# Scale pieces first in the prologue of a two-layer hybrid backbone step

## The chip, the cores and the metric

The kernel runs on one core of a Trainium2 chip. The metric is the device time of one execution in microseconds (us), lower is better. Engines are called as in the profile: PE is TensorE (PEld its weight loads), DVE is VectorE, ACT is ScalarE, POOL is GpSimd, SP is SyncE, which here only issues DMAs.

## What is computed

A trunk of two layers is applied to 512 latent tokens and 128 context tokens of width 1024. Each layer begins with an RMS norm whose result is scaled and shifted by a modulation (adaLN). The modulation is a vector of 6 x 1024 numbers per group of tokens, worked out from a small input vector by a matrix of 1024 x 6144:

```
mod = (jax.nn.silu(c) @ ada_w[l] + ada_b[l])[:, None, :]
xs, _ = _trunk_layer(xs, mod, layers[l], ctx)
```

Inside the layer the input of the first projection is, in effect, `rms_norm(x) * norm1_g * (1 + scale) + shift`, with shift the first 1024 and scale the second 1024 numbers of the modulation. DeltaNet, latent attention, window attention, an output projection and an MLP follow. The change touches only how this first modulation of layer 0 is made ready.

## The kernel before, in words

All matrix products of the layers are run as three products of rounded halves: a weight chunk `RAW` (128 x 2048) is rounded by ACT to `HI` (`split_hi`, L602) and DVE writes the rest `RAW - HI` to `LO` (`split_lo`, L927). The input is treated the same way: `X` is scaled by `GAIN` and rounded by ACT to `HH` (`norm_hi`, L607, two instructions for each of 8 tiles k: 128x512 for the latent tokens, 128x128 for the context tokens), and DVE writes `X * GAIN - HH` to `HL` (`norm_lo`, L934, again two instructions for each k). The shift does not go into X: it is one extra column at the end of `HH` and `HL` (`shift_hi` L614, `shift_lo` L944), so a projected tile brings its own bias. PE's `wstat` (L1409) multiplies; for its first tile it waits for the shift columns (semaphore `h_sl`), for the first `LO`, and before each k for `norm_lo` of that k (semaphore `h_lo`).

The modulation needed first (shift and scale of layer 0, 2048 numbers) comes in 8 pieces of 1 MB, `ADA`, 256 numbers each; pieces 0 to 3 are shift and 4 to 7 scale. For each piece j PE multiplies it (`ada_half`, L321, 16 matmul records), DVE copies the row from PSUM to `MODB` (L963), and PE turns the row into columns of PSUM bank 7 (`ada_turn`, L328, 4 records). PE's program runs `ada_half(j)` and then `ada_turn(j-1)`; `ada_half(j)` waits for the copy of j-1, which DVE signals by `pro_ev`. After the last turn DVE adds the bias (`ada_bias`, L334), makes `GAIN` (`ada_gain`, L339), and the normalised input follows.

POOL starts when X has landed and computes sums of squares of X for the RMS norm (`square_sum`: one L482, then seven pairs of L484 and L486, two SBUF inputs each), 15 instructions. Their result is used by PE only after its first tile.

Order is fixed by the program of each engine and by semaphores; nothing is scheduled by a table. All DMAs of this stretch are issued by SP in one queue in program order.

Of the kernel before, what the change touches and what calls it, by code (L numbers as in the profile page):

```python
# [15 lines left out]
KT = D // P  # L16
# [109 lines left out]
def build(nc, t):  # L126

    ctx = ExitStack()
    with ctx:
# [122 lines left out]
        def bank(i):  # L252
            return PS[:, i, :]
# [71 lines left out]
        def ada_turn(pe, rows, at_):  # L325

            for q in range(2):
                last = pe.matmul(bank(7)[:, 4 * at_ + 2 * q:4 * at_ + 2 * q + 2], rows[:, toks(q)], sel,  # L328
                                 start=True, stop=True)
            return last  # L330

        def ada_bias(lo, hi, vec):

            return nc.vector.tensor_tensor(MOD[:, lo:hi, :], bank(7)[:, 0:2 * (hi - lo)].rearrange("p (j g) -> p j g", g=2),  # L334
                                           vec.unsqueeze(2).broadcast_to([P, hi - lo, 2]), ALU.add)

        def ada_gain(q, sc, vec):

            return nc.vector.scalar_tensor_tensor(out=GAIN[:, q, :, :], in0=MOD[:, sc:sc + KT, :], scalar=1.0,  # L339
                                                  in1=vec.unsqueeze(2).broadcast_to([P, KT, 2]),  # L340
                                                  op0=ALU.add, op1=ALU.mult)

        pro_buf = [4, 5, 6, 7, 8, 0, 1, 2]
        blocks = [[LB if s == LB else (s if d == 0 else LB - 1 - s) for d in range(2)] for s in range(NB)]


# [3 lines left out]
        with nc.Block() as block:  # L350

            @block.sync
            def _(sp):
# [1 line left out]
                sp.dma_start(VA[:, :], t["va"][0]).then_inc(setup, 16)  # L355
                sp.dma_start(FG[:, :], t["fg"]).then_inc(setup, 16)
                for j in range(8):
                    if j == 2:
                        sp.dma_start(K[:, :], t["K"]).then_inc(k_in, 16)
                    if j == 3:  # L360
                        sp.dma_start(X[:, :, :, :], t["xT"]).then_inc(x_in, 16)
                    if j == 6:
                        sp.dma_start(RAW[0][:, :], t["ws"][0]).then_inc(raw_in[0], 16)
                    sp.dma_start(ADA[pro_buf[j]][:, :, :], t["ada"][0, j]).then_inc(pro_in[j], 16)
                sp.dma_start(RAW[1][:, :], t["ws"][1]).then_inc(raw_in[1], 16)

                def refill(g):
# [229 lines left out]
            def _(act):  # L597

                def split_hi(g):

                    act.wait_ge(raw_in[g % 2], 16 * (g // 2 + 1))
                    nc.scalar.copy(HI[g % 2][:, :], RAW[g % 2][:, :]).then_inc(hi_ready, 1)  # L602

                def norm_hi(q, k):

                    for g in range(2):
                        last = nc.scalar.activation(grp(HH[:, k, :, :], g), grp(X[:, k, :, :], g), ACT.Identity,  # L607
                                                    scale=GAIN[:, q % 2, k, g:g + 1])
                    last.then_inc(S["h_hi"], 1)

                def shift_hi(q):

                    lo = 3 * KT * (q % 2)
                    nc.scalar.copy(HH[:, :, 0, HT:W1], MOD[:, lo:lo + KT, :]).then_inc(S["h_sh"], 1)  # L614
# [7 lines left out]

                act.wait_ge(c_in, 16)
                nc.scalar.activation(SC[:, :, :], SC[:, :, :], ACT.Silu).then_inc(silu_c, 1)
                split_hi(0)
                act.wait_ge(k_in, 16)
                act.wait_ge(setup, 32)
                act.wait_ge(x_in, 16)
                act.wait_ge(pro_mod, 2)
                shift_hi(0)  # L630
                for k in range(KT):
                    norm_hi(0, k)
                for l in range(DEPTH):
                    o, g0 = base(l), l * CHUNKS

# [279 lines left out]
            def _(dve):  # L915
# [43 lines left out]
                for j in range(8):  # L959
                    dve.wait_ge(pro_mm, j + 1)  # L960
                    if j >= 2:
                        dve.wait_ge(pro_tr, j - 1)
                    nc.vector.tensor_copy(MODB[j % 2][:, :], bank(6)[:, j % 2 * AC:(j % 2 + 1) * AC]).then_inc(pro_ev, 1)  # L963
                    if j == 6:
                        split_lo(0)
                dve.wait_ge(pro_tr, 8)
                dve.wait_ge(setup, 32)
                ada_bias(0, 2 * KT, VA[:, 0:2 * KT]).then_inc(pro_mod, 1)
                dve.wait_ge(pro_mod, 1)
                ada_gain(0, KT, VA[:, 2 * KT:3 * KT]).then_inc(pro_mod, 1)  # L970
                shift_lo(0)
                dve.wait_ge(pro_mod, 2)
                for k in range(KT):
                    norm_lo(0, k)
                for l in range(DEPTH):
                    o, g0 = base(l), l * CHUNKS

# [412 lines left out]
            def _(pe):  # L1390
# [34 lines left out]
                    last.then_inc(nrb, 1)  # L1425

                pe.wait_ge(silu_c, 1)
                pe.wait_ge(k_in, 16)
                for j in range(9):
                    if j < 8:  # L1430
                        pe.wait_ge(pro_in[j], 16)
                        if j:
                            pe.wait_ge(pro_ev, j)
                        ada_half(pe, pro_buf[j], j).then_inc(pro_mm, 1)
                    if j:
                        pe.wait_ge(pro_ev, j)
                        ada_turn(pe, MODB[(j - 1) % 2], j - 1).then_inc(pro_tr, 1)
                used = [0] * 4
                for l in range(DEPTH):
                    o, g0, t0 = base(l), l * CHUNKS, l * TILES  # L1440
# [504 lines left out]
```

## Time and profile before

| what | value |
| --- | --- |
| time, median of 3 runs | 2066.24 us (2066.21 to 2070.67) |
| profiled execution: its own time | 2064.92 us |
| profiled execution: span in the trace | 2063.1 us |
| PE busy (share of the span) | 1954.9 us (95%) |
| DVE, ACT, POOL busy | 973.7, 663.7, 446.2 us |
| PE idle before its first `wstat` matmul | 5.22 us, first matmul at 45.43 us |

The span is the time from the first to the last record of the trace; the execution's own time is 1.8 us longer. PE is busy nearly always once the layers run. What matters here is the first 46 us, in which PE works little.

### The profile page before, as it was taken

The page shows a single profiled execution, that of the slowest core. Times are in us where ns is not written, and L with a number is a line of the kernel's source. Part 1 is how long each engine was busy: PE and PEld are TensorE (multiplying, and loading weights), DVE is VectorE, ACT ScalarE, POOL GpSimd, SP SyncE. Part 2 cuts the span into 40 slices and gives each one's busy share as a digit, 9 for nine tenths or more (in the row PEclk, how much of TensorE's full clock was granted, in tenths as well). Part 3 has the DMA queues.
Part 4 walks back from the last instruction along what each step waited for, and adds up shares of the span by engine and source line. Part 5 has one row for each costly group of instructions (what it writes and reads, how often), then busy time and mean ns, then how long its engine had stood idle before and what let it go on. Part 6 is the DMA issues. An engine that isn't in the chain of part 4 may idle for free. (4 is left out here: it accounts for less than half of the span.)

```text
span 2063.1 us, 32862 instructions
## 1 busy us (share of the span) xinstructions
PE 1954.9 (95%) x14279; PEld 1833.3 (89%) x14279; DVE 973.7 (47%) x1422; ACT 663.7 (32%) x1009; POOL 446.2 (22%) x326
## 2 busy tenths in 40 slices
PE   5999989897999999999999999989989999999996
PEld 3999966787999999999999998668879999999996
DVE  3445755677642323232555467457765332323223
ACT  2444246312322231312335432661122413122221
POOL 4000010342332030312430000013323403121144
PEclk9999999999999999999999999999999999999998
DMA  8444120101142222212254432010022122122111
GB/s 339 146 162 156 62 68 1 37 1 57 62 163 103 85 82 80 82 63 81 82 196 164 149 111 76 14 37 1 1 77 82 62 82 82 62 82 82 62 62 51
DMA packets 45630, 177.85 MB, mean 86 GB/s; under 512 B 21072, under 2 KB 22864, under 8 KB 26032
## 3 DMA queue, kind: packets, MB, share of 16 engines
q1 hardware_dynamic: 43952, 174.29, 23.9%
q8 instruction: 113, 1.85, 0.4%
q10 hardware_dynamic: 1536, 1.48, 0.2%
q14 instruction: 29, 0.24, 0.0%
HBM read 166.98 MB, written 8.68 MB: 85 GB/s over the span
## 5 line engine op out<-in xcount | busy, mean ns | idle before, releaser
L1409 PE MATMUL PS<-HH,HI 128*128 128x322 f32 (+1 forms) x1792 | 421.6, 317 | 5.2 <-DVE HL L934 5.2
L1409 PE MATMUL PS<-HL,HI 128*128 128x322 f32 (+1 forms) x1792 | 416.3, 314 | 0.0
L1409 PE MATMUL PS<-HH,LO 128*128 128x322 f32 (+1 forms) x1792 | 415.4, 313 | 0.0
L602 ACT CAST HI<-RAW 128x2048 fp32r<-128x2048 f32 x96 | 182.8, 1905 | 532.2 <-PE PS L1409 495.8
L1409 PEld LDWEIGHTS PS<-HH,HI 128*128 128x128 f32 x1792 | 304.5, 192 | 9.5 <-issue 9.4
L1409 PEld LDWEIGHTS PS<-HH,LO 128*128 128x128 f32 x1792 | 307.3, 192 | 0.0
L1409 PEld LDWEIGHTS PS<-HL,HI 128*128 128x128 f32 x1792 | 306.4, 192 | 0.0
L1409 PE MATMUL PS<-FH,HI 128*128 128x320 f32 x1280 | 292.9, 310 | 0.0
L1409 PE MATMUL PS<-FH,LO 128*128 128x320 f32 x1280 | 291.8, 309 | 0.0
L927 DVE TENSOR_TENSOR LO<-RAW,HI 128x2048 fp32r<-128x2048 f32 x96 | 231.7, 2414 | 105.6 <-ACT HI L602 105.6
L1409 PE MATMUL PS<-FL,HI 128*128 128x320 f32 x1152 | 263.2, 310 | 0.0
L583 POOL TENSOR_TENSOR TC<-TC 128x640 f32<-128x640 f32 x64 | 91.6, 1431 | 622.5 <-ACT FH L880 622.5
L956 DVE COPY BI<-PS 128x2 f32<-128x2 f32 x112 | 17.9, 160 | 425.7 <-PE PS L1409 412.9
L1409 PEld LDWEIGHTS PS<-FH,LO 128*128 128x128 f32 x1280 | 214.6, 188 | 0.0
L1409 PEld LDWEIGHTS PS<-FH,HI 128*128 128x128 f32 x1280 | 214.5, 189 | 0.0
L1335 DVE SCALAR_TENSOR_TENSOR X<-PS,MOD,X 128x512 f32<-128x512 f32 (+1 forms) x160 | 80.7, 546 | 262.1 <-PE PS L1409 262.1
L1409 PEld LDWEIGHTS PS<-FL,HI 128*128 128x128 f32 x1152 | 193.4, 188 | 0.0
L876 ACT ACTIVATE TC<-TMP,BI 128x512 f32<-128x512 f32 (+1 forms) x128 | 65.0, 555 | 201.1 <-DVE TMP L957 201.1
L586 POOL TENSOR_TENSOR FL<-TC,FH 128x640 fp32r<-128x640 f32 x64 | 100.1, 1564 | 5.0
L508 POOL COPY KTT<-KTT 32x1536 f32<-32x1536 f32 x2 | 4.0, 1982 | 448.8 <-DVE KTT L1129 448.8
L957 DVE TENSOR_TENSOR TMP<-PS,RB 128x640 f32<-128x640 f32 x112 | 91.3, 815 | 0.2 <-issue 0.2
L833 ACT COPY TT<-PS 128x512 f32<-128x512 f32 x40 | 21.7, 589 | 180.0 <-PE PS L1737 180.0
(270 smaller groups left out, 2458.5 us busy)
## 6 DMA issues: line engine op xcount, KB each, us to landing
RAW<-ws SPq DMA_DIRECT2D x96, 1024.0 KB, 4.8
ADA<-ada SPq DMA_DIRECT2D x48, 1024.0 KB, 5.0
X<-xT SPq DMA_DIRECT2D x1, 2560.0 KB, 16.5
X<-xT SPq DMA_DIRECT2D x2, 1280.0 KB, 5.7
xs<-X SPq DMA_DIRECT2D x1, 2560.0 KB, 8.4
X<-xs SPq DMA_DIRECT2D x2, 1280.0 KB, 5.9
yT<-YB SPq DMA_DIRECT2D x8, 320.0 KB, 2.2
ROT<-rot SPq DMA_DIRECT2D x2, 1024.0 KB, 4.8
```

The costliest lines, as they stand in the source:

```text
L508: nc.gpsimd.tensor_copy(KTT[64:QH, 1:H, 0:LAT], KTT[64:QH, 0:1, 0:LAT].broadcast_to([KR, H - 1, LAT])).then_inc(S["krc"], 1)
L583: nc.gpsimd.tensor_tensor(TC[u][:, 0:T], TC[u][:, 0:T], TC[u][:, 0:T], ALU.mult).then_inc(S["f1_sq"], 1)
L586: nc.gpsimd.tensor_tensor(flat(FL[:, e % 8, :, :]), TC[u][:, 0:T], flat(FH[:, e % 8, :, :]).bitcast(F32), ALU.subtract).then_inc(S["f1_lo" ...
L602: nc.scalar.copy(HI[g % 2][:, :], RAW[g % 2][:, :]).then_inc(hi_ready, 1)
L833: nc.scalar.copy(TT[d][:, :, :], bank(4 * d + 3).rearrange("p (h c) -> p h c", h=H)).then_inc(S["tcp"], 1)
L876: last = nc.scalar.activation(grp(TC[u][:, 0:T].rearrange("p (a b) -> p a b", a=2), g), grp(TMP[u][:, :, :], g), ACT.Relu, bias=BI[:, n % ...
L927: nc.vector.tensor_tensor(LO[g % 2][:, :], RAW[g % 2][:, :], HI[g % 2][:, :].bitcast(F32), ALU.subtract).then_inc(lo_ready, 1)
L956: nc.vector.tensor_copy(BI[:, n % 4, :], PS[:, 2 * (n % 2), HT:W1])
L957: nc.vector.tensor_tensor(TMP[n % 2][:, :, :], even(n % 2), RB[:, :, :], ALU.mult).then_inc(S["w_ev"], 1)
L1335: last = nc.vector.scalar_tensor_tensor(out=x, in0=grp(even(n % 2), g), scalar=MOD[:, gate + k, g:g + 1], in1=x, op0=ALU.mult, op1=ALU.add)
L1409: last = pe.matmul(bank(2 * u + a)[:, 0:e], w[:, cols], m[:, a, 0:e], start=(k == 0 and f), stop=(k == KT - 1 and e_))
```

## The change

The 8 pieces are loaded and worked through in the order 4, 5, 6, 7, 0, 1, 2, 3 (`pro_seq`), so scale comes before shift. X and the first weight chunk are both issued behind the fourth piece. DVE makes bias and gain of the scale part after the fourth turn, and puts `norm_lo` two at a time, and `split_lo(0)`, between its copies of the last four rows. ACT starts `norm_hi` when the gain is there and puts `split_hi(0)` in its middle. The shift part gets its own bias instruction at the end. PE waits for the constants `K` (which hold the selector matrix of the turns) only at its first turn.

```
         def ada_bias(lo, hi, vec):
 
-            return nc.vector.tensor_tensor(MOD[:, lo:hi, :], bank(7)[:, 0:2 * (hi - lo)].rearrange("p (j g) -> p j g", g=2),
+            at_ = 2 * lo if hi <= 2 * KT else 0
+            return nc.vector.tensor_tensor(MOD[:, lo:hi, :], bank(7)[:, at_:at_ + 2 * (hi - lo)].rearrange("p (j g) -> p j g", g=2),
                                            vec.unsqueeze(2).broadcast_to([P, hi - lo, 2]), ALU.add)
...
         pro_buf = [4, 5, 6, 7, 8, 0, 1, 2]
+        pro_seq = [4, 5, 6, 7, 0, 1, 2, 3]
...
                 for j in range(8):
-                    if j == 2:
+                    sp.dma_start(ADA[pro_buf[j]][:, :, :], t["ada"][0, pro_seq[j]]).then_inc(pro_in[j], 16)
+                    if j == 0:
                         sp.dma_start(K[:, :], t["K"]).then_inc(k_in, 16)
                     if j == 3:
                         sp.dma_start(X[:, :, :, :], t["xT"]).then_inc(x_in, 16)
-                    if j == 6:
                         sp.dma_start(RAW[0][:, :], t["ws"][0]).then_inc(raw_in[0], 16)
-                    sp.dma_start(ADA[pro_buf[j]][:, :, :], t["ada"][0, j]).then_inc(pro_in[j], 16)
                 sp.dma_start(RAW[1][:, :], t["ws"][1]).then_inc(raw_in[1], 16)
...
-                split_hi(0)
                 act.wait_ge(k_in, 16)
                 act.wait_ge(setup, 32)
                 act.wait_ge(x_in, 16)
                 act.wait_ge(pro_mod, 2)
+                for k in range(KT):
+                    if k == 4:
+                        split_hi(0)
+                    norm_hi(0, k)
+                act.wait_ge(pro_mod, 3)
                 shift_hi(0)
-                for k in range(KT):
-                    norm_hi(0, k)
...
+                    if j == 3:
+                        dve.wait_ge(pro_tr, 4)
+                        dve.wait_ge(setup, 32)
+                        ada_bias(KT, 2 * KT, VA[:, KT:2 * KT]).then_inc(pro_mod, 1)
+                        dve.wait_ge(pro_mod, 1)
+                        ada_gain(0, KT, VA[:, 2 * KT:3 * KT]).then_inc(pro_mod, 1)
+                        dve.wait_ge(pro_mod, 2)
+                    if j >= 4:
+                        norm_lo(0, 2 * (j - 4))
+                        norm_lo(0, 2 * (j - 4) + 1)
                     if j == 6:
                         split_lo(0)
                 dve.wait_ge(pro_tr, 8)
-                dve.wait_ge(setup, 32)
-                ada_bias(0, 2 * KT, VA[:, 0:2 * KT]).then_inc(pro_mod, 1)
-                dve.wait_ge(pro_mod, 1)
-                ada_gain(0, KT, VA[:, 2 * KT:3 * KT]).then_inc(pro_mod, 1)
+                ada_bias(0, KT, VA[:, 0:KT]).then_inc(pro_mod, 1)
+                dve.wait_ge(pro_mod, 3)
                 shift_lo(0)
-                dve.wait_ge(pro_mod, 2)
-                for k in range(KT):
-                    norm_lo(0, k)
...
                 pe.wait_ge(silu_c, 1)
-                pe.wait_ge(k_in, 16)
...
                         pe.wait_ge(pro_ev, j)
-                        ada_turn(pe, MODB[(j - 1) % 2], j - 1).then_inc(pro_tr, 1)
+                        if j == 1:
+                            pe.wait_ge(k_in, 16)
+                        ada_turn(pe, MODB[(j - 1) % 2], pro_seq[j - 1]).then_inc(pro_tr, 1)
```

On DVE, from the copy of the fourth row on, the program before reads as follows (the numbers behind the names tell buffers apart; MODB_115 and MODB_116 are the two row buffers):

```order
L963 COPY MODB_116<-PS 128x256
L963 COPY MODB_115<-PS 128x256
L963 COPY MODB_116<-PS 128x256
L963 COPY MODB_115<-PS 128x256
L927 TENSOR_TENSOR LO_55<-RAW_51,HI_53 128x2048
L963 COPY MODB_116<-PS 128x256
L334 TENSOR_TENSOR MOD<-PS,VA 128x32
L339 SCALAR_TENSOR_TENSOR GAIN<-MOD,VA 128x16
L944 TENSOR_TENSOR HL<-MOD,HH 128x8x2
L934 SCALAR_TENSOR_TENSOR HL<-X,GAIN,HH 128x2x256
```

On DVE after the change, from the same copy of the fourth row to the copy of the sixth:

```order
L966 COPY MODB_116<-PS 128x256
L335 TENSOR_TENSOR MOD<-PS,VA 128x16
L340 SCALAR_TENSOR_TENSOR GAIN<-MOD,VA 128x16
L966 COPY MODB_115<-PS 128x256
L937 SCALAR_TENSOR_TENSOR HL<-X,GAIN,HH 128x2x256
L937 SCALAR_TENSOR_TENSOR HL<-X,GAIN,HH 128x2x64
L937 SCALAR_TENSOR_TENSOR HL<-X,GAIN,HH 128x2x256
L937 SCALAR_TENSOR_TENSOR HL<-X,GAIN,HH 128x2x64
L966 COPY MODB_116<-PS 128x256
```

Four `norm_lo` instructions now stand between one copy and the next; the same four stand behind the next two copies, the second of them with `split_lo(0)` after it, and the last four behind the last copy.

On SP, the queue before, from the first piece to the second chunk (ADA_110 is the buffer of the first piece in order, RAW_51 the first weight chunk):

```order
L364 DMA ADA_110<-ada 128x2048
L364 DMA ADA_111<-ada 128x2048
L359 DMA K<-K 128x1924
L364 DMA ADA_112<-ada 128x2048
L361 DMA X<-xT 128x5120
L364 DMA ADA_113<-ada 128x2048
L364 DMA ADA_114<-ada 128x2048
L364 DMA ADA_106<-ada 128x2048
L363 DMA RAW_51<-ws 128x2048
L364 DMA ADA_107<-ada 128x2048
L364 DMA ADA_108<-ada 128x2048
L365 DMA RAW_52<-ws 128x2048
```

The same queue after the change:

```order
L360 DMA ADA_110<-ada 128x2048
L362 DMA K<-K 128x1924
L360 DMA ADA_111<-ada 128x2048
L360 DMA ADA_112<-ada 128x2048
L360 DMA ADA_113<-ada 128x2048
L364 DMA X<-xT 128x5120
L365 DMA RAW_51<-ws 128x2048
L360 DMA ADA_114<-ada 128x2048
L360 DMA ADA_106<-ada 128x2048
L360 DMA ADA_107<-ada 128x2048
L360 DMA ADA_108<-ada 128x2048
L366 DMA RAW_52<-ws 128x2048
```

X has moved behind one more piece, the first chunk ahead of two pieces more; the bytes ahead of the last piece are the same.

On PE the order of instructions does not change; the row of the fourth turn stands where it stood, behind the half of the fifth piece (ADA_114):

```order
L321 MATMUL PS<-ADA_113,SC 32x256 x8
L328 MATMUL PS<-K,MODB_115 128x2 x2
L321 MATMUL PS<-ADA_114,SC 32x256 x8
L328 MATMUL PS<-K,MODB_116 128x2 x2
L321 MATMUL PS<-ADA_106,SC 32x256 x8
```

The second turn shown here (MODB_116) is that of the fourth piece, for which the gain now waits.

## Rows read from the trace of the kernel before

**Rows 1.** The page: busy time of each engine, share of the span, instructions.

```profile
PE 1954.9 (95%) x14279; PEld 1833.3 (89%) x14279; DVE 973.7 (47%) x1422; ACT 663.7 (32%) x1009; POOL 446.2 (22%) x326
```

**Rows 2.** Timeline of PE: start us, duration us, group, [idle before <- releaser].

```profile
33.19 1.94 PE L321 MATMUL PS<-ADA,SC 128*32 128x256 f32 x16 [1.45 <-DMA ADA<-ada]
35.05 1.01 PE L328 MATMUL PS<-K,MODB 128*128 128x2 f32 x4
39.20 1.01 PE L328 MATMUL PS<-K,MODB 128*128 128x2 f32 x4 [0.33 <-DVE MODB L963]
45.43 0.88 PE L1409 MATMUL PS<-HH,HI 128*128 128x322 f32 x2 [5.22 <-DVE HL L934]
```

**Rows 3.** Timeline of ACT, 28 to 60 us.

```profile
30.69 1.90 ACT L602 CAST HI<-RAW 128x2048 fp32r<-128x2048 f32 x1 [27.42 <-DMA RAW<-ws]
41.67 0.21 ACT L614 CAST HH<-MOD 128x16 fp32r<-128x16 f32 x1 [9.09 <-DVE GAIN L339]
41.78 7.34 ACT L607 ACTIVATE HH<-X,GAIN 128x512 fp32r<-128x512 f32 x16
```

**Rows 4.** Timeline of DVE, 34 to 60 us, and its instruction at 42.91 alone.

```profile
35.53 3.28 DVE L927 TENSOR_TENSOR LO<-RAW,HI 128x2048 fp32r<-128x2048 f32 x1
38.73 0.41 DVE L963 COPY MODB<-PS 128x256 f32<-128x256 f32 x1
40.25 0.19 DVE L334 TENSOR_TENSOR MOD<-PS,VA 128x32 f32<-128x32 f32 x1 [1.10 <-PE PS L328]
40.48 1.09 DVE L339 SCALAR_TENSOR_TENSOR GAIN<-MOD,VA 128x16 f32<-128x16 f32 x1
41.91 0.98 DVE L944 TENSOR_TENSOR HL<-MOD,HH 128x16 fp32r<-128x16 f32 x1 [0.35 <-ACT HH L614]
42.91 8.86 DVE L934 SCALAR_TENSOR_TENSOR HL<-X,GAIN,HH 128x512 fp32r<-128x512 f32 x16
51.68 2.28 DVE L927 TENSOR_TENSOR LO<-RAW,HI 128x2048 fp32r<-128x2048 f32 x1
42.91 2.12 DVE L934 SCALAR_TENSOR_TENSOR HL<-X,GAIN,HH 128x512 fp32r<-128x512 f32 x1
```

**Rows 5.** Timeline of POOL, 20 to 45 us.

```profile
20.78 1.25 POOL L482 TENSOR_TENSOR SQA<-X 128x640 f32<-128x640 f32 x1 [20.33 <-DMA X<-xT]
36.74 3.18 POOL L484 TENSOR_TENSOR TC<-X 128x640 f32<-128x640 f32 x1
40.00 1.53 POOL L486 TENSOR_TENSOR SQA<-SQA,TC 128x640 f32<-128x640 f32 x1
41.61 1.25 POOL L484 TENSOR_TENSOR TC<-X 128x640 f32<-128x640 f32 x1
42.94 1.53 POOL L486 TENSOR_TENSOR SQA<-SQA,TC 128x640 f32<-128x640 f32 x1
```

**Rows 6.** Timeline of DVE and POOL later in the program.

```profile
543.33 1.25 POOL L484 TENSOR_TENSOR TC<-X 128x640 f32<-128x640 f32 x1 [3.81 <-DVE X L1335]
544.34 0.79 DVE L934 SCALAR_TENSOR_TENSOR HL<-X,GAIN,HH 128x512 fp32r<-128x512 f32 x1 [1.16 <-ACT HH L607]
544.34 2.37 DVE L934 SCALAR_TENSOR_TENSOR HL<-X,GAIN,HH 128x512 fp32r<-128x512 f32 x2 [1.16 <-ACT HH L607]
544.66 1.89 POOL L486 TENSOR_TENSOR SQA<-SQA,TC 128x640 f32<-128x640 f32 x1
1010.82 3.49 POOL L486 TENSOR_TENSOR SQA<-SQA,TC 128x640 f32<-128x640 f32 x1
1012.81 2.31 DVE L934 SCALAR_TENSOR_TENSOR HL<-X,GAIN,HH 128x512 fp32r<-128x512 f32 x2
```

**Rows 7.** Busy time in two windows of the first tile, with granted clock (PEclk).

```profile
core 0: us, PE busy (x) PEld busy (x) DVE busy (x) ACT busy (x) POOL busy (x), PEclk, DMA share, GB/s
45.40:51.20 5.80, 5.77 (x22) 5.80 (x23) 5.80 (x13) 5.51 (x10) 0.00 (x0) 1.00 0.72 302
51.20:55.20 4.00, 4.00 (x27) 4.00 (x27) 2.77 (x3) 0.00 (x0) 2.04 (x2) 1.00 0.20 29
```

## The prediction, made before the changed kernel ran

> **What bounds the kernel now.** The page comes first: PE is busy 95% of the span [rows 1], so time is won or lost where PE waits. The timeline of PE then shows where that is in the stretch of the change: its last turn runs from 39.20 to 40.21, and its first real matmul starts at 45.43, after 5.22 us of waiting for a `norm_lo` [rows 2]. From there it runs without a gap. So what the change is worth is the shift of that one start, 45.43.
>
> What stands between the last piece and that start is read from the timelines of ACT, DVE and POOL. `ada_half` of the seventh piece starts when that piece lands, 33.19; the first chunk, one place ahead in the queue, lands at 30.69 [rows 2, 3]. So 1 MB takes 2.5 us. I take the transfers of this queue to run back to back at that pace, so that where a piece lands follows from its place in the queue. The eighth lands by 35.7. Its row is copied at 38.73 only, because `split_lo(0)` holds DVE from 35.53 on; then come turn (to 40.21), bias 0.19, gain 1.09, `shift_hi` 0.21, `shift_lo` 0.98 and the first `norm_lo` 2.12 and 0.26 [rows 3, 4].
>
> The reader is to see that three of these durations are not work. The gain is issued at 40.48 and ends at 41.57, just behind a POOL instruction that ends at 41.53. `shift_lo` ends at 42.89 behind one that ends at 42.86. The first `norm_lo` ends at 45.03, 0.56 behind one that ends at 44.47. The other way round, `split_lo(0)` ends at 38.81 and the POOL instruction under way from 36.74 takes 3.18 in place of 1.25 [rows 4, 5]. The bias and the copies, which read PSUM and at most one SBUF tensor, are not held. So DVE instructions with two SBUF inputs and POOL's take turns, each waiting for the whole of the other. POOL is done at 44.5; seven and a half of the eight `norm_lo` run behind that, free, at 0.93 us for each k (45.29 to 51.77), well ahead of PE.
>
> Who goes next when both want to is read further on. At 544.34 DVE issues the two instructions of a `norm_lo`. The first goes when POOL's ends at 544.58, POOL's next (issued 544.66) follows and ends at 546.55, and DVE's second ends at 546.71: it waited for all of POOL's. At 1010.82 a POOL instruction waits behind a `split_lo`; it then runs to 1014.31 ahead of a `norm_lo` pair issued at 1012.81, which takes 2.31 [rows 6]. A waiting POOL instruction gets in between any two of DVE's.
>
> **The change, step by step.** Landings: cvec to the eighth piece are the same bytes. K, X and the chunk change places with pieces. X lands one piece later, so POOL starts at 20.78 + 2.5 = 23.3. The chunk lands at about 25.7, pieces five to eight at 28.2, 30.7, 33.2, 35.7, the last as before.
>
> *The gain.* The first four pieces (scale) are in at about 17 (28.2 less a piece 2.5, the chunk 2.5 and X, 2.5 MB, 6.2) and their rows copied at about 20. But PE's program puts the fourth turn behind the half of the fifth piece, which lands at 28.2. A turn ends 2.87 behind the start of the half in front of it (33.19 to 36.06 [rows 2]): 31.1. The gain is issued at 31.3 and waits for a POOL instruction that ends at 31.6 (the L484 three pairs ahead of the one at 36.74 began at 36.74 - 3 x 2.95 = 27.89; + 2.5 + 1.25 [rows 5]). So the gain is there at 31.7, 9.9 ahead of 41.57; that is what the change brings.
>
> *What is now put between the copies.* On POOL are left from 31.7 on one L486 and four pairs L484/L486. Each pair takes 2.95 undisturbed (from the end of L482 at 22.0 to 36.74 are five pairs). A 128x512 `norm_lo` taking its turn costs POOL 1.89 - 1.53 = 0.35 [rows 5, 6] and the second none; so in contention one k takes 2.95 + 0.35 = 3.3 in place of 0.93. ACT starts `norm_hi` at 31.8 at 0.92 each (7.34 / 8 [rows 3]), fast enough.
>
> - Copy 5 at 31.8 to 32.2 (its row is there at 30.2); half 6 at 32.3, its row at 34.3.
> - `norm_lo` 0: POOL's L486 ends at 33.3, pair one gives 33.8 for the first instruction and 35.1 for the second. `norm_lo` 1: 3.3 later, 38.4.
> - Copy 6 at 38.4 to 38.8, 4.1 behind its row. As `ada_half` of the next piece waits for this copy, half 7 starts at 38.9, though its piece landed at 33.2.
> - `norm_lo` 2 and 3 wait for POOL first (39.9), two more cycles: 45.0. Copy 7 to 45.5, half 8 at 45.6, its row at 47.5.
> - `norm_lo` 4: POOL's last ends at 46.5, then free: 47.3; `norm_lo` 5: 48.2; `split_lo(0)` without POOL (2.28, as the one at 51.68 [rows 4]): 50.4.
> - Copy 8 to 50.8, turn 50.9 to 51.9. That is 11.7 behind 40.21.
> - Behind the last turn less is left: `norm_lo` 6 and 7 end at 52.6, shift bias 52.8, `shift_hi` 53.1, `shift_lo` 53.3 with POOL gone (some 0.2, by the bias's 0.19). PE starts 0.1 later at 53.4. That tail is 1.5 where it was 5.2.
>
> Sum: + 11.7 - 3.7 = + 8.0 us; the start goes from 45.4 to 53.4. The one added bias costs 0.2 and is in it. K's wait moved behind the first half lets PE begin earlier at the very start only, where it next waits for pieces anyway: nothing.
>
> *What hangs behind.* `split_hi(1)` and `split_lo(1)` follow 4 us after the start and are wanted only two tiles later. SP's refill waits for `split_lo(0)` (now 50.4, before 38.8), and queued behind it are the parameters and the next two `ADA` loads, some 5 us each; they are wanted after the first tile (before: 55.2 [rows 7], now 63). POOL's sums end at 46.5 and are wanted at 63. All covered. So everything after moves by the same 8.0. Cover lost anywhere here would cost at most what is late: the parameters would have to land over 7 us later than the 56 expected.
>
> *Clock.* In the first 5.8 us of the first tile PE finishes 22 matmuls in 5.77, or 0.262 each; then 27 in 4.00, or 0.148, at a granted clock of 1.00 in both windows [rows 7]. So the first matmuls run at about half speed, that is, as at 1.2 GHz, the lower of the clock's two levels, though the column says 1.00. Before the start PE had idled 5.2 us; after the change it idles 1.5 us with a thin pattern ahead. I take the same slow stretch. If it were gone, 5.8 us of work would take 3.3: 2.5 less. If the rest of the tile (27 matmuls) were slow too: 3.1 more.
>
> **A rule beside the row.** The row gives 3.3 us for one contended k: POOL's pair of 2.95 and 0.35 for the DVE instruction that took its turn, since the two overlap at their edges [rows 5, 6]. The Trainium skill, page "SBUF — State Buffer", section "Who interferes with whom", speaks against this change: a DVE instruction with two SBUF inputs and a GpSimd one that reads SBUF exclude each other for their whole length. Taken at its word, a contended k is the sum of both engines' durations, 2.95 + 0.93 = 3.9, and the four contended ones add 2.3 us more: a start at 55.7, + 10.3, where the row gives + 8.0. The row decides.
>
> **Bounds of the contention.** Low: DVE keeps the port while it has instructions and POOL waits, rival one. High: from 31.7 on nothing overlaps: all of POOL's remaining work (1.5 + 4 x 2.8 = 12.7), DVE's 16 `norm_lo` 7.4, `split_lo(0)` 2.3, four copies 1.7 and the shift part 0.7 add up to a start at 56.5, + 11.1. I take 8.0, since the rows at 544 and 1010 show the turn-taking itself.
>
> **Rivals.**
> - *DVE keeps its turn.* For it: in the back-to-back stretch before, instructions of DVE overlap by a few hundredths, so that POOL may not get in. Against: both places in rows 6. Then each `norm_lo` pair takes 1.9 to 2.7 with at most one POOL instruction between copies: copies 6, 7, 8 at 34.9, 37.8, 43.3; last turn to 44.8; `norm_lo` 6 and 7 and `shift_lo` behind POOL's rest: start at 48.1, + 2.7 us, 2068.9.
> - *The work is hidden, as the change wants.* The place is the gap of 2.5 us between two copies (half 1.94 and turn 1.01 less a copy 0.41). If POOL does not get in the way and `split_lo(0)` fits too, the last turn ends at about 39.4 and only bias, `shift_hi`, and `shift_lo` (waiting once for POOL) are left: start at 41.0, - 4.4 us, 2061.8. It decides once the four `norm_lo` instructions between copies take under 2.5; they take 1.9 free and 6.6 in turns. Against it is also `split_lo(0)`, which alone outgrows the gap.
> - *Clock.* As the main case, but PE starts fast: + 5.5, 2071.7.
>
> **How the numbers follow.** Turn-taking as worked out 0.72, DVE keeps its turn 0.12, hidden 0.06, clock 0.10. The sum is made in the profiled execution: 2064.92 + 8.0 = 2072.9 there (span 2071.1). The median of the runs is 1.3 above it, so 2066.24 + 8.0 = 2074.2. Range: the high end is the bound of + 11.1, 2077.3, rounded up to 2077.5; the low end takes in the first rival with little to spare, 2067.5; left out are the hidden case and the tails, under 0.2. About what a measurement of this kernel can tell from no change is 0.3%, 6.2 us. The main case lies 1.8 above that, and I give it 9 in 10 to stay above: 0.65, and 0.01 of the clock case for slower; the rest, with both other rivals, is same; faster by over 6.2 would need more than the hidden case gives: 0.02.
>
> **What would show it.** Right: gain at about 31.7; `norm_lo` instructions of 1.2 to 1.7 us each alternating with POOL's until 46 or 47; copies at 38.4, 45.0 and 50.4; PE's fourth, sixth and seventh waits inside the prologue ended by DVE's copies, not by DMAs; first `wstat` matmul at 53.4. Wrong: copies 6 and 7 on time at 34 and 37, POOL's instructions stretched in DVE's place, or the gain at 20 (if the fourth turn were not held by the fifth piece). A first matmul at 0.148 each from the start would show the clock case.

## The result, and the profile after

The changed kernel takes 2073.09 us (median of 22 runs, 2066.62 to 2082.78), the kernel before 2066.22 us in the same series (22 runs, 2056.1 to 2074.59). The ratio is 1.0032 with a 95% interval of 1.0019 to 1.0045: slower by 6.6 us, 3.9 to 9.3. The profiled execution took 2072.92 us with a span of 2071.1. Ratios here and below leave out slow executions; there was one, of the spread version, of 8153.11 us.

Of the timeline of PE in the changed kernel these are the rows from the fifth piece on that end a wait; they answer to [rows 2].

```profile
28.04 1.94 PE L321 MATMUL PS<-ADA,SC 128*32 128x256 f32 x16 [7.56 <-DMA ADA<-ada]
32.06 1.94 PE L321 MATMUL PS<-ADA,SC 128*32 128x256 f32 x16 [1.15 <-DVE MODB L966]
38.61 1.94 PE L321 MATMUL PS<-ADA,SC 128*32 128x256 f32 x16 [3.67 <-DVE MODB L966]
45.15 1.93 PE L321 MATMUL PS<-ADA,SC 128*32 128x256 f32 x16 [3.66 <-DVE MODB L966]
50.47 1.01 PE L328 MATMUL PS<-K,MODB 128*128 128x2 f32 x4 [2.44 <-DVE MODB L966]
52.92 0.90 PE L1417 MATMUL PS<-HH,HI 128*128 128x322 f32 x2 [1.44 <-DVE HL L947]
...
62.40 1.17 PE L1425 MATMUL PS<-K,SQA 128*128 128x1 f32 x10
```

Before, what PE's halves waited for from there on was a landing piece (1.45 us at 33.19 [rows 2]). Now only the half at 28.04 waits for one. The three behind it, and the last turn, wait for a copy on DVE (1.15, 3.67, 3.66, 2.44 us). The last turn ends at 51.48 where it ended at 40.21, the first `wstat` matmul starts at 52.92 in place of 45.43, 7.5 us later. The sums of squares, the first thing after the first tile, come at 62.40.

The timeline of DVE, for [rows 4]:

```profile
31.16 0.29 DVE L340 SCALAR_TENSOR_TENSOR GAIN<-MOD,VA 128x16 f32<-128x16 f32 x1
31.49 0.42 DVE L966 COPY MODB<-PS 128x256 f32<-128x256 f32 x1
32.62 5.51 DVE L937 SCALAR_TENSOR_TENSOR HL<-X,GAIN,HH 128x512 fp32r<-128x512 f32 x4 [0.71 <-ACT HH L608]
38.05 0.41 DVE L966 COPY MODB<-PS 128x256 f32<-128x256 f32 x1
38.39 6.28 DVE L937 SCALAR_TENSOR_TENSOR HL<-X,GAIN,HH 128x512 fp32r<-128x512 f32 x4
44.59 0.41 DVE L966 COPY MODB<-PS 128x256 f32<-128x256 f32 x1
44.93 2.95 DVE L937 SCALAR_TENSOR_TENSOR HL<-X,GAIN,HH 128x512 fp32r<-128x512 f32 x4
47.80 2.28 DVE L930 TENSOR_TENSOR LO<-RAW,HI 128x2048 fp32r<-128x2048 f32 x1
50.00 0.41 DVE L966 COPY MODB<-PS 128x256 f32<-128x256 f32 x1
50.33 1.93 DVE L937 SCALAR_TENSOR_TENSOR HL<-X,GAIN,HH 128x512 fp32r<-128x512 f32 x4
```

The four `norm_lo` instructions (two k) take 5.51 and 6.28 us while POOL works, 2.95 where POOL ends in their midst, 1.93 when it is gone. From 32.62 to 52.3 DVE is never idle. The timeline of POOL, for [rows 5]:

```profile
23.08 1.25 POOL L483 TENSOR_TENSOR SQA<-X 128x640 f32<-128x640 f32 x1 [22.63 <-DMA X<-xT]
...
33.13 1.58 POOL L485 TENSOR_TENSOR TC<-X 128x640 f32<-128x640 f32 x1
34.79 1.54 POOL L487 TENSOR_TENSOR SQA<-SQA,TC 128x640 f32<-128x640 f32 x1
36.40 1.58 POOL L485 TENSOR_TENSOR TC<-X 128x640 f32<-128x640 f32 x1
...
44.60 1.54 POOL L487 TENSOR_TENSOR SQA<-SQA,TC 128x640 f32<-128x640 f32 x1
```

L485 starts at 33.13, 36.40, 39.68 and 42.94, every 3.27 us; undisturbed it was every 2.95. Of DVE's instructions two, taken alone, show the turns (start, duration):

```profile
34.78 2.09 DVE L937 SCALAR_TENSOR_TENSOR HL<-X,GAIN,HH 128x512 fp32r<-128x512 f32 x1
...
36.79 1.33 DVE L937 SCALAR_TENSOR_TENSOR HL<-X,GAIN,HH 128x128 fp32r<-128x128 f32 x1
```

The first, 128x512, was started at 34.78, just before POOL's L487 at 34.79, and took 2.09: it ends at 36.87, 0.54 behind POOL's end at 36.33. The second, 128x128, took 1.33 and ends at 38.12, 0.14 behind the end of L485 (36.40 + 1.58). Each waited until a POOL instruction had ended; 0.75 and 0.34 are their durations with POOL gone.

### The profile page after: what moved, and what is told of

Read it like the earlier page. It is cut to its first block and busy times, and to the rows that moved or that the text cites. A ratio compares the mean times of both kernels' runs of the same rounds, so it can differ in the third digit from the quotient of the medians.

```text
span 2071.1 us, 32864 instructions
## 1 busy us (share of the span) xinstructions
PE 1955.8 (94%) x14279; PEld 1834.5 (89%) x14279; DVE 979.7 (47%) x1423; ACT 663.8 (32%) x1009; POOL 446.4 (22%) x326
## 5 line engine op out<-in xcount | busy, mean ns | idle before, releaser
L321 PE MATMUL PS<-ADA,SC 128*32 128x256 f32 x768 | 58.3, 426 | 26.1 <-DMA ADA<-ada 17.6
```

Of the source, the lines that this page charges most:

```text
L321: last = pe.matmul(bank(6)[q:q + 32, j % 2 * AC:(j % 2 + 1) * AC], SC[:, k, :], ADA[buf][:, k, :], start=(k < 4), stop=(k >= 4))
```

## Experiments

Ten kernels in twelve runs. In each one the start of the first `wstat` matmul (before 45.43, changed 52.92) is what is compared; it and the rows around it are read in one trace. Transfers mostly land up to 0.4 us earlier or later from trace to trace, so a difference of that size is not read as an effect. The time of a single run says little either, as the last section shows.

### POOL's sums held back in the changed kernel

```
                 pool.wait_ge(x_in, 16)
+                pool.wait_ge(S["h_sl"], 1)
                 square_sum(0, lambda k: flat(X[:, k, :, :]))
```

> The changed kernel, with POOL's sums of squares of X held until shift_lo of the first norm is done; nothing else is moved. Theory (turn-taking between POOL and DVE makes the copies late): norm_lo pairs take 1.9 us between copies in place of 5.5 to 6.3, copies 6, 7, 8 come at about 34, 37 and 42, the last turn ends at 43.5 and the first wstat matmul starts at 45.2 in place of 52.9. Rival (DVE's own added work is what makes the copies late, POOL is no matter): the start stays at 52 to 53. In either case PE then waits some 13 us after its first tile for the sums, which end only at about 69, so the whole kernel is not faster than the changed one: about 2078.

DVE's timeline of this kernel:

```profile
32.77 1.94 DVE L938 SCALAR_TENSOR_TENSOR HL<-X,GAIN,HH 128x512 fp32r<-128x512 f32 x4 [0.71 <-ACT HH L609]
34.63 0.42 DVE L967 COPY MODB<-PS 128x256 f32<-128x256 f32 x1
34.97 1.93 DVE L938 SCALAR_TENSOR_TENSOR HL<-X,GAIN,HH 128x512 fp32r<-128x512 f32 x4
37.18 0.42 DVE L967 COPY MODB<-PS 128x256 f32<-128x256 f32 x1 [0.29 <-PE PS L321]
...
42.26 0.42 DVE L967 COPY MODB<-PS 128x256 f32<-128x256 f32 x1
```

The `norm_lo` groups take 1.94 and the copies come at 34.6, 37.2 and 42.3. The first `wstat` matmul starts at 45.18, as the theory said to 0.02 us. PE then waits 14.32 us for the sums, and the one run took 2083.9 us (about 2078 expected). Without POOL the changed prologue is only as good as the old one with POOL. That does not put the whole 7.5 us down to POOL, since the old one was held up by it too: see the run with POOL held back in the kernel before, where the loss is divided.

### The turn of the fourth piece early

```
                 for j in range(9):
+                    if j == 4:
+                        pe.wait_ge(pro_ev, 4)
+                        ada_turn(pe, MODB[1], pro_seq[3]).then_inc(pro_tr, 1)
                     if j < 8:
                         pe.wait_ge(pro_in[j], 16)
...
-                    if j:
+                    if j and j != 4:
                         pe.wait_ge(pro_ev, j)
```

That is the second form. In the first, the turn stood behind `pe.wait_ge(pro_in[j], 16)` and the wait for `pro_ev` that follows it.

> The changed kernel, with PE's turn of the fourth piece put ahead of the half of the fifth, so that the gain no longer waits for a piece that lands at 28. Both theories: gain at about 20.9 in place of 31.4. Theory (DVE with its port waits is the bound from 31 on): norm_lo still stands behind copy 5, which comes 1.1 us earlier, so the start moves from 52.9 to about 51.7 only. Rival (the late gain is what spoils the change): the start follows the gain by up to 10 us, to 43 to 46.

In the first form the turn ran at 27.94, behind the wait for the fifth piece, and the gain ended at 30.05: the edit did not do what it was meant to. The start moved to 52.64.

> The changed kernel, with PE's turn of the fourth piece now ahead of the wait for the fifth piece too (in the first attempt it stood behind that wait and moved by one half only). Gain at about 20.9, ACT's norm_hi from X's landing at 23 on. Theory (from copy 5 on DVE and POOL share one port, and their work adds up): copy 6 at 36.8, copy 7 at 43.3, but POOL's sums then end as late as before and take from norm_lo 4 and 5 what was won; start at 52.4, 0.5 below the changed kernel. Rival (the late gain is what spoils the change): start at 43 to 46.

Mended, the gain ended at 22.06, 9.4 us ahead of the changed kernel. The start was 52.87, unchanged within 0.05 (expected 52.4), and the one time 2075.15. X landed 0.3 us later in this trace (POOL began at 23.37, not 23.08), so some 0.3 of the 0.5 forecast may be there. DVE's timeline shows why:

```profile
21.89 0.17 DVE L340 SCALAR_TENSOR_TENSOR GAIN<-MOD,VA 128x16 f32<-128x16 f32 x1
...
37.02 0.41 DVE L966 COPY MODB<-PS 128x256 f32<-128x256 f32 x1
37.36 6.28 DVE L937 SCALAR_TENSOR_TENSOR HL<-X,GAIN,HH 128x512 fp32r<-128x512 f32 x4
43.56 0.41 DVE L966 COPY MODB<-PS 128x256 f32<-128x256 f32 x1
43.90 3.94 DVE L937 SCALAR_TENSOR_TENSOR HL<-X,GAIN,HH 128x512 fp32r<-128x512 f32 x4
...
49.96 0.41 DVE L966 COPY MODB<-PS 128x256 f32<-128x256 f32 x1
```

Copies 6 and 7 come 1.0 us earlier than in the changed kernel, but the group behind copy 7 takes 3.94 in place of 2.95, and copy 8 is at 49.96 in place of 50.00. POOL's sums end when they end (46.8 and 46.1); what DVE does ahead of that, it pays for. The rival, a late gain, falls for the changed kernel: the gain came 9.4 us earlier and 0.3 us at most followed.

### The `norm_lo` back behind `shift_lo`

```
-                    if j >= 4:
-                        norm_lo(0, 2 * (j - 4))
-                        norm_lo(0, 2 * (j - 4) + 1)
...
                 shift_lo(0)
+                for k in range(KT):
+                    norm_lo(0, k)
```

> The changed kernel, with the eight norm_lo put back behind shift_lo; order of loads, early gain and early norm_hi stay. Theory (what stands between the copies does the harm): copies come on their rows, copy 8 at about 40.5, the last turn ends at 41.7, POOL still overlaps until 46 to 47, the start is at 45 to 46, as before the change. Rival (the new order of the loads, with X one piece later, does the harm): the start stays above 50.

Copy 8 came at 39.74, the last turn ended at 41.47, the start was at 44.67, a little under the 45 to 46 expected and 0.8 ahead of the kernel before. The order of the loads is not what does the harm. But the eight `norm_lo` now took 11.10 us (before 8.86 [rows 4]), since POOL worked on until 47.64 (before 44.47); PE ran dry once more in its first tile:

```profile
44.67 0.87 PE L1416 MATMUL PS<-HH,HI 128*128 128x322 f32 x2 [3.20 <-DVE HL L937]
47.85 0.90 PE L1416 MATMUL PS<-HH,HI 128*128 128x322 f32 x2 [1.23 <-DVE HL L937]
```

and the sums came at 56.62, 1.3 us behind the kernel before (55.35). Its single time, 2078.59, is above what that explains: at the mark that stands at 203.03 in the trace before (explained in the last section) it was 2.8 us behind, at the one at 551.15 it was 11.5, so most of it arose later.

### `split_lo(0)` behind the last copy

```
-                    if j == 6:
+                    if j == 7:
                         split_lo(0)
```

> The changed kernel, with split_lo(0) moved from ahead of copy 8 to behind it and the last four norm_lo. Theory (DVE is busy or held without a gap from 32.6 to 52.3, so only the sum of its work counts): copy 8 comes at about 47.8 in place of 50.0, but the start stays at 52.9 within 0.3. Rival (the late last row and its turn set the start): the start comes 2.2 us earlier, at 50.7.

Copy 8 came at 47.75, 2.25 us earlier, the last turn ended at 49.24, and the start stayed at 52.87. So the late copies of the changed kernel are a sign, not the cause: DVE's work and the turns it waits for add up without a gap, and its last instruction sets the start.

### X and K first, in the kernel before and in the changed one

```
+                sp.dma_start(X[:, :, :, :], t["xT"]).then_inc(x_in, 16)
+                sp.dma_start(K[:, :], t["K"]).then_inc(k_in, 16)
                 for j in range(8):
...
-                        sp.dma_start(K[:, :], t["K"]).then_inc(k_in, 16)
...
-                        sp.dma_start(X[:, :, :, :], t["xT"]).then_inc(x_in, 16)
```

> The kernel before the change, with X and then K loaded ahead of the first piece; nothing else is moved. POOL's sums then run from about 11 to 33 and are done before split_lo(0), gain, shift_lo and norm_lo. Theory (POOL's turn-taking is on the path before, too): split_lo(0) 2.3 in place of 3.28, gain 0.3 in place of 1.09, shift_lo 0.2 in place of 0.98, first norm_lo 0.75 in place of 2.12; the last piece lands as before, at 35.7; the first wstat matmul starts at 41.6 in place of 45.4, and the time falls by 3.8 us. Rival (these waits are covered by something else): the start stays at 45 and the time is the same.

POOL now ended at 33.2. DVE's timeline of the kernel before with X first:

```profile
35.90 2.28 DVE L925 TENSOR_TENSOR LO<-RAW,HI 128x2048 fp32r<-128x2048 f32 x1
38.37 0.42 DVE L961 COPY MODB<-PS 128x256 f32<-128x256 f32 x1 [0.19 <-PE PS L321]
40.13 0.19 DVE L334 TENSOR_TENSOR MOD<-PS,VA 128x32 f32<-128x32 f32 x1 [1.34 <-PE PS L328]
40.36 0.17 DVE L339 SCALAR_TENSOR_TENSOR GAIN<-MOD,VA 128x16 f32<-128x16 f32 x1
40.88 0.18 DVE L942 TENSOR_TENSOR HL<-MOD,HH 128x16 fp32r<-128x16 f32 x1 [0.35 <-ACT HH L612]
41.88 7.49 DVE L932 SCALAR_TENSOR_TENSOR HL<-X,GAIN,HH 128x512 fp32r<-128x512 f32 x16 [0.82 <-ACT HH L605]
```

`split_lo(0)` took 2.28 (3.28), the gain 0.17 (1.09), `shift_lo` 0.18 (0.98), each as the theory had it or better. The start was 43.04, not 41.6: 2.4 us gained, not 3.8. Three things were missed. Piece seven landed 0.36 us later than before (its half began at 33.55, not 33.19), and the last half with it (36.37, not 35.99). With copy 8 on time, the last turn queues on PE behind the one before it (8 records in 1.87 us, to 40.10), so the last turn ended only 0.1 ahead of the 40.21 of before. And the first `norm_lo` waits 0.82 for ACT's first `norm_hi`, which was hidden behind `shift_lo` held by POOL. The ratio to the kernel before was 0.9983 (0.9963 to 1.0002). A second series:

> The kernel before with X and K first, once more, beside the spread version on the same chip: start at 43.0, time 2.4 to 2.9 us below the kernel before, 1.5 above the spread version if that starts at 41.5.

Start at 42.90, the ratio 0.9990 (0.9970 to 1.0011); the medians, 2064.15 and 2063.13 for the kernel before, stand the other way round. The difference is in the trace both times and under what the times can show.

> The changed kernel, with X and K loaded ahead of the first piece. POOL is done at about 33, so only the first norm_lo meets it. Theory: start at about 45.3, the time 7.6 us below the changed kernel and that of the kernel before within 1 us; so without any contention the change still gives nothing, because DVE's own work between the copies (1.9 and 4.1 us against gaps of 2.5) makes them late, and against the kernel before with X first it loses 3.7 us. Rival (contention was all that spoiled the change): start at 41 or earlier, time below 2062.5.

The start was 46.95: 6.0 us ahead of the changed kernel, but 1.5 behind the kernel before and 3.9 behind the same loads in the old order of work. (1.2 of the distance from the expected 45.3 is the gain, which met POOL's last instruction and took 1.45.) The ratio was 1.0011 (0.9992 to 1.0031), and the median 2065.9 us against 2059.91 for the old order with X first in the same series. DVE met POOL no more in its `norm_lo`, and in the trace the change still lost against the old order. The first two gaps held their 1.9 us of work (copy 7 came as soon as its row was there); the third did not hold 0.58 of waiting for ACT, 1.9 and 2.3, so copy 8 came at 44.03, 2.3 behind its row, and the last four `norm_lo` stand ahead of the shift.

### POOL held back in the kernel before

```
                 pool.wait_ge(x_in, 16)
+                pool.wait_ge(S["h_lo"], KT)
```

> The kernel before the change, with POOL's sums of squares held until the eighth norm_lo of the first norm is done, loads as they were. Theory: the same four waits go, and the start moves from 45.4 to about 41.5 even with X landing late, so that it is POOL and not the place of X in the queue. Rival (the place of X in the queue matters by itself): the start stays at 45. Either way PE waits about 19 us for the sums after its first tile, so the kernel is slower.

The gain took 0.17, `shift_lo` 0.18, `split_lo(0)` 2.28, again. The start was 43.87, less than hoped; the last piece landed late in this run (the half waited 0.88 us for it and began at 37.19, before 35.99), and from the start of that half to the first `wstat` matmul are 6.68 us, where it was 9.44 and, with X first, 6.67 (36.37 to 43.04). So holding POOL back and loading X first give the same; it is POOL, not the place of X. PE waited 20.69 us for the sums; the one time was 2089.56.

With this the 7.5 us can be divided. Without POOL the changed kernel started at 45.18. The kernel before without POOL would have started at 42.67, had its last half begun at 35.99 as before (an estimate: 35.99 + 6.68). So sharing with POOL costs the changed kernel 7.7 us (52.92 less 45.18) and the kernel before 2.8 (45.43 less 42.67): 5.0 more. The other 2.5 (45.18 less 42.67) are the new order of DVE's work itself.

### Work spread by what the gaps hold

X and K first as above, scale first, the early turn, and:

```
                 nc.scalar.activation(SC[:, :, :], SC[:, :, :], ACT.Silu).then_inc(silu_c, 1)
+                split_hi(0)
...
                         ada_gain(0, KT, VA[:, 2 * KT:3 * KT]).then_inc(pro_mod, 1)
+                        split_lo(0)
                         dve.wait_ge(pro_mod, 2)
-                    if j >= 4:
-                        norm_lo(0, 2 * (j - 4))
-                        norm_lo(0, 2 * (j - 4) + 1)
-                    if j == 6:
-                        split_lo(0)
+                    for k in {4: (0,), 5: (1, 2), 6: (3, 4), 7: (5,)}.get(j, ()):
+                        norm_lo(0, k)
...
                 shift_lo(0)
+                norm_lo(0, 6)
+                norm_lo(0, 7)
```

> X and K first, scale pieces first, the turn of the fourth piece ahead of the fifth half, split_hi(0) ahead of norm_hi, split_lo(0) right behind the gain, then one, two, two and one norm_lo behind copies 5, 6, 7, 8, and the last two behind shift_lo, where PE's slow start hides them. Theory (each gap between copies holds about 2.5 us of DVE work, and what does not fit there goes behind the start): gain at about 27.4, copies within 1 us of their rows, last turn ends at 39.8, start at 40.6 to 41.5, the time 4 to 5 us below the kernel before (about 2061.5). Rival (the copies are made late again): start above 43.

This had the turn in its first form, behind the wait for the fifth piece. Gain at 30.10, start at 43.31, ratio 1.0000 (0.9980 to 1.0020). That is the rival's number (above 43), but not for its reason alone: copies 5 and 6 were 0.9 and 0.7 us behind their rows, copies 7 and 8 on time, and the gain was 2.7 us late, since the early turn was missing.

> The spread version with the turn of the fourth piece ahead of the wait for the fifth. Theory: gain at 26 to 27, copies 5 to 8 within 1 us of their rows, last turn ends near 40.7, start at 41.5, 1.8 below the first spread version and 3.9 below the kernel before; the time 3.9 us below the kernel before. Rival (POOL's last two or three instructions and split_lo(0) still push copy 5 and all behind it): start at 43 as in the first version.

```profile
28.53 1.94 PE L321 MATMUL PS<-ADA,SC 128*32 128x256 f32 x16 [0.44 <-DMA ADA<-ada]
...
37.64 1.93 PE L321 MATMUL PS<-ADA,SC 128*32 128x256 f32 x16 [0.33 <-DVE MODB L964]
39.51 1.87 PE L328 MATMUL PS<-K,MODB 128*128 128x2 f32 x8
42.16 0.90 PE L1415 MATMUL PS<-HH,HI 128*128 128x322 f32 x2 [0.78 <-DVE HL L945]
...
51.18 1.06 PE L1423 MATMUL PS<-K,SQA 128*128 128x1 f32 x9
```

Gain at 28.53, two later than expected: the first half begins only at 16.18, when its piece has landed behind X and `K`, and four halves and turns follow it nearly without a gap; copies within 1 us of their rows; the last turn ends at 41.38, the start is at 42.16 (expected 41.5), the sums at 51.18: 3.3 and 4.2 us ahead of the kernel before. Ratio 0.9982 (0.9962 to 1.0003). Run once more:

> The mended spread version once more, for its time. Theory: start at 42.2 and end of the first tile at 51.2 again, 4.2 us ahead of the kernel before, and the time 3 to 4 us below it (ratio 0.998 to 0.9985). Rival (what is won in the first 55 us is lost again further on): ratio within 0.0005 of 1.

Start at 42.17, the sums at 51.89; ratio 0.9991 (0.9974 to 1.0008), medians 2062.56 and 2066.22 us; the end of the first tile was 3.5 us ahead, not 4.2, and the ratio lies between what the theory and the rival had. Both intervals lie below that of the changed kernel (1.0019 to 1.0045), so this version beats it. Against the kernel before the trace shows 3.3 us in the start, and the times can't tell it from nothing. The rival is not ruled out: the last section follows the lead through the traces.

## Why the prediction was right

The forecast was 2074.2 us and + 8.0; measured were 2073.09 and + 6.9 between the medians. By its steps:

- **Landings and gain.** Right. X's first use at 23.08 (23.3), the half of the fifth piece at 28.04 (28.2), gain at 31.45 (31.7).
- **Turn-taking.** Right, and the size too: 3.27 us for a contended k (3.3). The 128x512 `norm_lo` costs POOL 0.33 and the 128x128 one nothing. Only the sign for it was drawn too narrow: single instructions took 0.98 to 2.09 us with their waits, not 1.2 to 1.7. The Trainium skill's reading in the prediction (page "SBUF — State Buffer", section "Who interferes with whom"), with both durations in full, gave 3.9 and a start at 55.7. That two-input instructions exclude each other agrees with the trace; that their whole durations add does not (3.27, not 3.9), since they overlap by their edges.
- **Copies and last turn.** 38.05, 44.59, 50.00 and 51.48 (38.4, 45.0, 50.4, 51.9): the difference of 0.4 is there from copy 6 on, and 0.25 of it from the first `norm_lo`, which found POOL's instruction ending at 33.05, not 33.3.
- **The tail.** 1.44 (1.5).
- **The sum.** The start moved by 7.5 (8.0). The first tile took 9.48 in place of 9.92, so its end moved by 7.05. The medians differ by 6.9, but their agreement with this is partly luck: the interval of 3.9 to 9.3 would hold 5 or 8 as well.
- **The bounds and rivals.** DVE does not keep its turn. The hidden case was reached by no kernel tried. From the start of the last half to the end of the last turn passed 3.73 us with X first and 3.74 in the spread version, so a turn ending at 39.4 needs that half to start with its piece, at 35.7. In the spread version, the best one, it waited for copy 7 and began at 37.64; the start was 42.16.

What the prediction had in the wrong light is the path. It followed the late copies from piece to piece, as if PE and DVE passed a delay to and fro. Moving `split_lo(0)` took 2.25 us from the last copy and nothing from the start, and a gain 9.4 us earlier gave 0.3 at most: from 32.6 on the bound is DVE with its turns. The steps summed right because they listed all of DVE's work anyway.

That the span of the profiled execution came out at just the forecast 2071.1 is chance: the first tile ended 7.05 later, POOL's first `UU` at 378.90 before came at 388.42 (+ 9.5), and the first L483 of the third norm 8.2 later.

## What to carry to other kernels

Work that is moved into another engine's gaps is priced by what it meets there, not by what it took where it stood: here `norm_lo` went from a place behind POOL's sums to one beside them and each k took 3.3 us for 0.93. Ask of every DVE instruction with two SBUF inputs what POOL does at that time; it may be cheaper to let POOL begin earlier (its input first in the queue: the start 2.4 us earlier here, without touching the work) than to move DVE's. And when an instruction that is ready is queued behind one that waits for a transfer, the wait stands in the program's order: look at which wait comes ahead of it, as the first form of the early turn showed.

## What the runs showed that was not expected

**PE's clock in the prologue.** With X first, PE's halves run from 16 us on with hardly a gap. In three of the six traces with that order a half then took 1.07 in place of 1.94: the changed kernel with X first, the first spread version, and the second run of the mended one, whose first run did not show it. So it is not fixed by the kernel. In the changed kernel with X first:

```profile
21.35 1.07 PE L321 MATMUL PS<-ADA,SC 128*32 128x256 f32 x16 [0.21 <-DMA ADA<-ada]
23.84 1.94 PE L321 MATMUL PS<-ADA,SC 128*32 128x256 f32 x16 [0.89 <-DMA ADA<-ada]
```

Its windows show the fall in the granted clock (the column before the last two):

```profile
core 0: us, PE busy (x) PEld busy (x) DVE busy (x) ACT busy (x) POOL busy (x), PEclk, DMA share, GB/s
19.00:20.50 1.50, 1.47 (x16) 0.68 (x16) 0.00 (x0) 0.00 (x0) 1.42 (x2) 1.00 1.00 421
20.50:23.20 2.70, 2.25 (x28) 1.46 (x24) 0.85 (x2) 0.00 (x0) 2.54 (x3) 1.00 1.04 434
23.20:26.00 2.80, 2.16 (x18) 0.89 (x18) 0.16 (x1) 0.00 (x0) 2.64 (x3) 0.56 1.01 421
26.00:35.00 9.00, 4.61 (x36) 2.80 (x39) 2.76 (x5) 1.50 (x3) 7.24 (x8) 0.50 1.01 421
```

The clock is at 1.00 (2.4 GHz) while 28 matmul records fit in 2.25 us, and at 0.50 (1.2 GHz) from 26 on. In the kernel before with X first the same column says 1.00 throughout, while its halves take 1.93:

```profile
20.50:23.20 2.70, 2.70 (x24) 1.52 (x20) 0.43 (x1) 0.00 (x0) 2.54 (x3) 1.00 1.01 425
26.00:35.00 9.00, 8.39 (x64) 4.56 (x60) 1.27 (x3) 1.90 (x1) 7.05 (x8) 1.00 1.01 422
```

So in these traces the granted clock of the profile shows a fall only behind a first rise; ahead of that the duration of a known instruction has to be read. The mean granted clock of this trace, 0.973 against 0.979 before, is then no sign of a slower layer: some 27 us at about 0.50 (0.51 from 23.20 to 46.95, 0.52 from there to 51.00) in a span of 2063 take 0.0065 off the mean, an estimate. The same trace bears out what the prediction took from rows 7 for the first tile: its pairs of matmuls that take 0.74 us (47.00 to 49.00) run at 0.50, those that take 0.46 (51.00 to 56.00) at 1.00.

**The slow beginning of the first tile.** From its first matmul to the sums it took 9.92 us before and 9.48 after, 8.57 with `split_lo(0)` moved, 9.99 with the first form of the early turn, 9.02 and 9.72 in two runs of one kernel (the mended spread version). The point from which a pair of matmuls takes 0.46 in place of 0.74 us comes at no fixed distance from the start, and is worth 1.4 us between the extremes; the prediction's bounds of - 2.5 and + 3.1 held.

**Spread between runs.** The kernel before ranged from 2055.74 to 2075.26 us over its series, with mean granted clocks of 0.966 to 0.983. That spread is larger than any effect in this study, so only the mean of many runs can show one. The traces show where it arises. A mark that can be found in each is the `split_hi` that stands at 203.03 in the trace before:

```profile
203.03 1.90 ACT L602 CAST HI<-RAW 128x2048 fp32r<-128x2048 f32 x1 [7.27 <-PE PS L1409]
210.09 1.90 ACT L603 CAST HI<-RAW 128x2048 fp32r<-128x2048 f32 x1 [7.27 <-PE PS L1417]
```

The second row is of the changed kernel: 7.06 us later, as the end of the first tile was 7.05 later. In the kernel before with X first the mark is at 200.20, in the two traces of the spread version at 198.88 and 199.59: 2.8, 4.2 and 3.4 us ahead, as the end of their first tile was. So what the prologue wins or loses is carried unchanged for 150 us, at a granted clock of 1.00 (window 55.40 to 203.00 before).

Then the traces drift apart where the granted clock is lower. From the mark to POOL's first `UU` the kernel before takes 175.87 us at a granted clock of 0.96, the changed one 178.33 at 0.94. From there to the `split_hi` at 551.15 the kernel before takes 172.25 at 0.96, the changed one 172.39 at 0.96, X first 174.82 at 0.94, the spread version 174.10 and 175.06 at 0.95 and 0.94. At that `split_hi` the leads of 2.8, 4.2 and 3.4 us have become - 0.2, 0.7 and 0.3. All six traces with X first took 174.1 to 178.5 there; of the eight with X later five took 172.2 to 172.4, three 174.9 to 178.5. Whether loading X first costs something there, or chance does, stays open. By the end of the span the scatter has gone on: X first is 5.9 us shorter than the kernel before, the two traces of the spread version 3.1 longer and 0.3 shorter. With kernels that differ in one place of the program, the marks of one trace at that place say more than the times, but they don't show that the whole execution is shorter by as much.
